# Feed-forward part of a decoder layer: up and down projection in one block, glu split into own buffers, last k steps by row tile

## What is computed

```python
def conv_glu_ffn(xn, w_up, conv_w, conv_b, w_down):
    h = causal_dwconv(xn @ w_up, conv_w) + conv_b      # 3 taps
    gate, val = jnp.split(h, 2, axis=-1)
    return (jax.nn.silu(gate) * val) @ w_down
...
        x = h + conv_glu_ffn(rms_norm(h, norm2_w[l]), ...)
    return rms_norm(x, final_norm_w)
```

## Time and profile before

| | us |
|---|---|
| median of 3 runs | 1781.9 |
| lowest, highest | 1780.5, 1782.3 |
| profiled execution: span | 1780.5 |
| profiled execution: its time, the lowest of the three | 1780.5 |
| TensorE busy in the span | 1693.2 (95%) |
| VectorE, ScalarE, GpSimd busy | 687.8, 494.3, 514.9 |

### The profile page before, as it was taken

How to read it: one execution, slowest core, us unless ns; L and a number is a source line. 1 busy time by engine, 2 the same in 40 slices (tenths; PEclk the granted TensorE clock), 3 DMA queues, 4 the chain that set the end, 5 groups by cost and what they waited for, 6 DMA issues and landing times. The chain is left out here.

```text
span 1780.5 us, 21145 instructions
## 1 busy us (share of the span) xinstructions
PE 1693.2 (95%) x8339; PEld 1408.3 (79%) x8339; DVE 687.8 (39%) x938; ACT 494.3 (28%) x617; POOL 514.9 (29%) x316
## 2 busy tenths in 40 slices
PE   6999999999999999996999789999999999799996
PEld 4788888887888888885788668888888888688885
DVE  4223223354454544642642313332222222345445
ACT  4322221222222343332221222222222222223223
POOL 4235231312213123212142322222222221344444
PEclk9999999999999999998899889999999999899998
DMA  4232422121121324432760111111111110311113
GB/s 156 60 95 71 136 82 58 40 56 53 48 67 44 91 79 112 132 117 102 253 235 34 62 48 47 47 47 47 48 54 51 47 47 24 130 50 50 47 47 124
DMA packets 173546, 139.64 MB, mean 78 GB/s; under 512 B 20420, under 2 KB 153004, under 8 KB 173484
## 3 DMA queue, kind: packets, MB, share of 16 engines
q1 hardware_dynamic: 173264, 138.67, 25.2%
q10 hardware_dynamic: 220, 0.09, 0.0%
HBM read 106.39 MB, written 32.34 MB: 78 GB/s over the span
## 5 line engine op out<-in xcount | busy, mean ns | idle before, releaser
L409 PE MATMUL acc<-xh,w_high 128*128 128x512 f32 x1504 | 486.3, 404 | 7.9 <-PEq L1376 7.9
L409 PE MATMUL acc<-xl,w_high 128*128 128x512 f32 x1504 | 468.8, 392 | 0.0
L409 PE MATMUL acc<-xh,w_low 128*128 128x512 f32 x1504 | 467.2, 391 | 0.0
L409 PEld LDWEIGHTS acc<-xl,w_high 128*128 128x128 f32 x1504 | 284.2, 189 | 61.1
L409 PEld LDWEIGHTS acc<-xh,w_low 128*128 128x128 f32 x1504 | 283.7, 189 | 61.4
L409 PEld LDWEIGHTS acc<-xh,w_high 128*128 128x128 f32 x1504 | 272.9, 190 | 64.1 <-issue 15.8
L1730 DVE SCALAR_TENSOR_TENSOR u_conv<-acc,prm,u_conv 128x1023 f32<-128x1023 f32 x88 | 112.8, 1282 | 341.1 <-ACT u_conv L1693 334.8
L779 POOL TENSOR_TENSOR w_low<-w_raw,w_high 128x1024 fp32r<-128x1024 f32 x49 | 117.0, 2388 | 376.5 <-ACT w_high L853 376.5
L1717 POOL TENSOR_TENSOR w_low<-w_raw,w_high 128x1024 fp32r<-128x1024 f32 x42 | 101.0, 2404 | 363.3 <-ACT w_high L1675 363.3
L1869 DVE TENSOR_TENSOR w_low<-w_raw,w_high 128x512 fp32r<-128x512 f32 x42 | 104.9, 2497 | 129.3 <-ACT w_high L1833 129.3
L1854 POOL TENSOR_TENSOR xl<-glu,xh 128x1024 fp32r<-128x1024 f32 x44 | 105.2, 2393 | 156.8 <-ACT xh L1830 131.6
(11 more groups left out here) (288 smaller groups left out, 2182.4 us busy)
## 6 DMA issues: line engine op xcount, KB each, us to landing
w_raw<-in_w_in_dram SPq DMA_DIRECT2D x51, 512.0 KB, 4.5
w_raw<-in_w_up_dram SPq DMA_DIRECT2D x44, 512.0 KB, 3.8
w_raw<-in_w_down_dram SPq DMA_DIRECT2D x44, 256.0 KB, 2.6
conv_d<-so SPq DMA_DIRECT2D x16, 512.0 KB, 3.0
gate_d<-qk SPq DMA_DIRECT2D x16, 512.0 KB, 3.1
g_gates<-gate_d SPq DMA_DIRECT2D x8, 1024.0 KB, 5.6
qk<-in_x_dram SPq DMA_DIRECT2D x8, 512.0 KB, 8.3
ckqk<-conv_d SPq DMA_DIRECT2D x8, 512.0 KB, 5.1
```

The lines of the kernel that those rows point to most:

```text
L409: mm = nc.tensor.matmul(out[:, lo:hi], w, xx[:, lo:hi], start=first and j == 0, stop=last and j == 2)
```

## The change

The functions `ffn`, `ffn_up`, `ffn_down` and `down_slots` become one `ffn` with one block.

- The order in which the operands of the down steps are prepared is a list `prep` of 44 (half, kk); `pos` gives a step's number in it, counted from 1: half 0's steps are 1 to 22, half 1's steps 0 to 13 are 23 to 36, and then steps 14 to 17 alternate with 18 to 21.
- `gh` and `gl` get buffers of their own (two slots each); the tail's (half 1, steps 18 to 21) lie in `xh`. The weights have four slots of a quarter of the ring each; the tail's lie in consumed tiles of `glu`. The rows of h lie in the memory of `xl`.
- ScalarE makes `gh` of steps 0 and 1 ahead of its last turn of up, and their weights' high parts inside it. VectorE makes their low parts between the two tap groups of the last turn.
- TensorE does steps 0 and 1 first on the row tiles whose banks are free (4 to 7, then 0 and 1), then on 2 and 3, and raises `s_k` for step 0 only then. Steps 18 to 21 of half 1 are done row tile by row tile, 12 matmuls each.
- The weights' split stands ahead of the glu split of the same number in ScalarE's queue; before, it stood behind. VectorE makes the low parts up to number `pos[(1, 2)]` = 25 ahead of half 0's additions.
- The squares of half 0's 512 columns go in ScalarE's queue at steps 2 to 9 of half 1, the product of these columns with the norm weight in GpSimd's at steps 6 to 13. At the end the square and VectorE's scaling are of 512 columns; ScalarE scales the other 512. Each row tile is stored in two halves.
- All loops over down steps are written out on all five engines.

```diff
+    prep = [(0, kk) for kk in range(FT)] + [(1, kk) for kk in range(BODY - GROUP)]
+    for pair in zip(lead, tail):
+        prep += pair
+    pos = count(prep)
...
+        gh2 = sb(ctx, "f_gh", [P, 2, S], F32R)
+        gl2 = sb(ctx, "f_gl", [P, 2, S], F32R)
...
+        def wait_used(eng, n):
+            if n == FT - 1:
+                eng.wait_ge(s_bank, NT)
+            else:
+                eng.wait_ge(s_k, n + 1 if n < FT else n)
...
             def _(sp):
...
+                for p in range(1, len(prep) + 1):
+                    load(p)
+                    if 5 <= p < 5 + NT:
+                        st = p - 5
+                        if st == 0:
+                            sp.wait_ge(s_acc, 2 * FT)
+                        sp.dma_start(h[st], h_d[...]).then_inc(s_h, 16)
...
+                for st in range(NT):
+                    sp.wait_ge(s_y2, st + 1)
+                    sp.dma_start(rows[:, 1, :], h[st][:, 1, :]).then_inc(s_out, 16)
+                    sp.wait_ge(s_y, st + 1)
+                    sp.dma_start(rows[:, 0, :], h[st][:, 0, :]).then_inc(s_out, 16)
...
             def _(act):
...
+                def glu_high(p):
+                    half, kk = prep[p - 1]
+                    n = half * FT + kk
+                    if half == 0:
+                        act.wait_ge(s_glu, kk + 1)
+                    if (half, kk) not in tail and n >= 2:
+                        wait_used(act, n - 2)
...
+                    nc.scalar.activation(gh(half, kk), glu[:, kk, :], ACT.Copy).then_inc(s_gh, 1)
...
+                glu_high(1)
+                glu_high(2)
                 turn(FT - 1, last=True)
+                for p in range(3, len(prep) + 1):
+                    down_high(p)
+                    glu_high(p)
+                    if prep[p - 1][0] == 1 and 2 <= prep[p - 1][1] < 2 + NT:
+                        square(0, prep[p - 1][1] - 2)
+                for st in range(NT + 1):
+                    if st < NT:
+                        square(1, st)
+                    if st:
+                        scale_first(st - 1)
...
             def _(pool):
...
+                for p in range(1, len(prep) + 1):
+                    pool.wait_ge(s_gh, p)
+                    nc.gpsimd.tensor_tensor(gl(half, kk), glu[:, kk, :], gh(half, kk).bitcast(F32),
+                                            ALU.subtract).then_inc(s_gl, 1)
+                    if half == 1 and 6 <= kk < 6 + NT:
...
+                        nc.gpsimd.tensor_tensor(h[st][:, 0, :], h[st][:, 0, :], fw[:, 0, :], ALU.mult).then_inc(s_first, 1)
...
             def _(dve):
...
+                taps(FT - 1, 0)
+                down_low(1)
+                down_low(2)
+                taps(FT - 1, 1)
+                gated(FT - 1)
+                early = pos[(1, 2)]
+                for p in range(3, early + 1):
+                    down_low(p)
+                dve.wait_ge(s_h, 16 * NT)
+                for st in range(NT):
+                    add(0, st)
+                for p in range(early + 1, len(prep) + 1):
+                    down_low(p)
...
+                for st in range(NT + 2):
+                    if st < NT:
+                        add(1, st)
+                    if 1 <= st <= NT:
+                        mean_square(st - 1)
+                    if st >= 2:
+                        scale_second(st - 2)
...
             def _(pe):
...
+                free = [st for st in range(NT) if st not in (2, 3)]
+                for kk in range(2):
+                    ready(0, kk)
+                    for st in sorted(free, key=lambda st: (st < 4, st)):
+                        if kk == 0 and st == 0:
+                            pe.wait_ge(s_taken, 2 * FT - 1)
+                        down(0, kk, st)
+                pe.wait_ge(s_taken, 2 * FT)
+                for kk in range(2):
+                    for st in (2, 3):
+                        mm = down(0, kk, st)
+                    mm.then_inc(s_k, 1)
...
+                            if half and kk == 0:
+                                pe.wait_ge(s_sum, st + 1)
+                            mm = down(half, kk, st)
...
+                for st in range(NT):
+                    for _, kk in tail:
+                        mm = down(1, kk, st)
+                    mm.then_inc(s_bank, 1)
```

More of the change, by code:

```diff
@@ L1624, in _ @@
                 transposes(NT - 1)
[L1627 to L1637, removed]
@@ L1649, in ffn_up @@
     with ExitStack() as ctx:
+        glu_at = nc.sbuf_base
+        glu = sb(ctx, "glu", [P, FT, S])
         cv = sb(ctx, "u_conv", [P, 2, S])
         sg = sb(ctx, "u_silu", [P, S])
+        gh2 = sb(ctx, "f_gh", [P, 2, S], F32R)
+        gl2 = sb(ctx, "f_gl", [P, 2, S], F32R)
+        ss0 = sb(ctx, "f_ss0", [P, 8])
+        FW_TILE, W_TILE = 2, 4
+        rows_of_h = nc.alloc_sbuf_tensor_at("f_h", [P, NT, NHALF, HALF], F32, offset=xl_at)
+        h = [rows_of_h[:, st] for st in range(NT)]
+        last_w = nc.alloc_sbuf_tensor_at("f_last_w", [P, GROUP, 2, HALF], F32R, offset=glu_at + W_TILE * S * 4)
@@ L1695, in turn @@
                         if j == 0:
-                            if not last:
+                            if last:
+                                down_high(1)
+                                down_high(2)
+                            else:
                                 split(i + 1, 0)
@@ L1741, in turn, with down_low @@
                                             ALU.mult).then_inc(s_glu, 1)
[L1743 to L1748, removed]
+                def down_low(p):
+                    half, kk = prep[p - 1]
+                    dve.wait_ge(s_dhi, p)
+                    nc.vector.tensor_tensor(dlo(half, kk), draw(p), dhi(half, kk).bitcast(F32),
+                                            ALU.subtract).then_inc(s_dlo, 1)
@@ L1761, in turn, with down, ready @@
                         mm.then_inc(s_acc, 1)
+                def down(half, kk, st):
+                    rows = slice(st * P, (st + 1) * P)
+                    a, b = gh(half, kk), gl(half, kk)
+                    for n, (x, w) in enumerate(((a, dhi(half, kk)), (a, dlo(half, kk)), (b, dhi(half, kk)))):
+                        mm = nc.tensor.matmul(every[st], x[:, rows], w, start=kk == 0 and n == 0,
+                                              stop=kk == FT - 1 and n == 2)
+                    return mm
+                def ready(half, kk):
+                    pe.wait_ge(s_gl, pos[(half, kk)])
+                    pe.wait_ge(s_dlo, pos[(half, kk)])
                 turn(0, True)
@@ new lines, in _ @@
+                for half in range(NHALF):
+                    for kk in range(0 if half else 2, BODY if half else FT):
+                        ready(half, kk)
+                        for st in range(NT):
+                            if half and kk == 0:
+                                pe.wait_ge(s_sum, st + 1)
+                            mm = down(half, kk, st)
+                            if not half and kk == FT - 1:
+                                mm.then_inc(s_bank, 1)
+                        if half or kk < FT - 1:
+                            mm.then_inc(s_k, 1)
```

289 lines of the change are left out of this document (122 added, 167 removed).

## The result

The changed kernel takes 1772.7 us (median of 4 runs, 1768.8 to 1773.2) against 1781.6 (median of 4 runs of the kernel before); the ratio is 0.9947, with a 95% interval of 0.9935 to 0.9958. That is faster by 0.5%, and 8.9 us against the 9.8 that the sum gave.

The account below looks back on a forecast made before the run. TensorE never rests inside the down projection, so only the joints can move: -10.4 + 1.7 + 5.1 + 1.9 - 8.1 = -9.8, from 1781.9 to 1772.1 us; own range 1769 to 1775, 8-in-10 range 1765 to 1777.

Parts of the forecast that it names:

- The turn: From up to down projection: no wait there, a new gap of 2.56 us before step 2; 10.4 us less.
- The clock in this gap: Slow TensorE clock from the new gap before step 2: 1.7 us more, bounds 0 and 3.4.
- The half change: From half 0 to half 1: TensorE waits behind ScalarE's weight split, VectorE's low part and first addition; 5.1 us more.
- The clock behind it: Half clock after the wait between half 0 and half 1: 1.9 us lost, bounds 0 and 3.4.
- The rival without this wait: Half 0 to half 1: no stall, as number 25's weights are split earlier; 1765.1 us, chance 0.07.
- Half 1: Norm work added to ScalarE and GpSimd during half 1 costs TensorE nothing: 0 us.
- The worst case for GpSimd and VectorE in the last pairs: Last prepared pairs: VectorE held through two GpSimd instructions, a low part late; 3 us kept as bound, 0 taken.
- The end: After the last matmul: 7.4 us to the end of the span instead of 15.5; 8.1 us less.
- The rival on the slower side: Down's written-out matmul stream: instructions come too slowly, pitch 0.24 us adds 14.0 us; 1786.1 us, chance 0.03.

Follow-up runs that it names:

- The two cuts: Changed kernel with VectorE's additions put before low part 25, 1763.7 us; or with ScalarE splitting weights 25 ahead of glu split 24, 1764.0 us.
- step 0 whole: Changed kernel, but TensorE does step 0 on all eight row tiles before step 1; 1768.5 us.
- tail by step: Changed kernel, but the last four k steps of half 1 go step by step over all row tiles; 1776.3 us.
- norm whole at the end: Changed kernel, but squares, scaling and store of all 1024 columns at the end, no norm work in half 1; 1773.4 us.
- late glu split: Changed kernel, but the glu splits of steps 0 and 1 stand behind ScalarE's last turn of up; 1775.3 us.

## Why the prediction was right

- **The turn.** Right. Step 2 starts 13.1 us behind up's last evacuation; the prediction had 1526.05 - 1512.82 = 13.2. The wait before it was 2.28 as recorded and 1526.14 - 1523.70 = 2.44 by slots, for 2.56 worked out from slots. One reading was off: 1536.48 is a time of the chain, whose pieces follow each other without the overlap of the matmuls. In the timeline the third step of the kernel before starts at 1536.32 (row below), so the forecast for the turn was worth 10.3 and not 10.4. The experiment with step 0 done whole shows that the late step counter is the cause of the wait.
- **The clock in this gap.** The term of 1.7 was 1.6 in the profiled run, but as a sure loss it was wrong, and that it came out is in part luck: the same wait was followed by half clock in four profiled runs and by full clock in two. The Trainium skill, page "TensorE: Matmul & The Clock Gate", section "What's actually happening", has the gate go by recent activity on a free-running beat; the six runs agree with that in so far as the same wait had either outcome, 14 or 21 matmuls behind it. The changed kernel's lowest run (1768.8, granted clock 0.982, the others 0.980) may have been spared too, but it has no trace, and it lies 4 us under the others, more than this one stretch can give.
- **The half change.** Right in mechanism and size: a wait of 4.96 by slots for 5.1, with each row of the chain in the forecast order. The two cuts show it. The clock behind it cost 2.5, not 1.9: the half clock lasted until 1646.9, 5.2 us behind the restart, where the row that the term came from had 3.7. This term is the largest miss of the sum. The rival without this wait, which had 0.07, is out.
- **Half 1.** Nothing was forecast and nothing was lost; the windows with and without the moved norm work are alike (115.1 us busy of 115.1, x509 both times). The worst case for GpSimd and VectorE in the last pairs (3 us) did not occur.
- **The end.** 7.3 us behind the last matmul for 7.4 forecast, so 8.2 less instead of 8.1. The chain was right to 0.3 us (the last store is issued at 4.1, not 4.4, since an issue took 0.33 to 0.52 and not 0.61). What the prediction did not say, and the experiments show, is which part pays: the spacing of the tiles.
- **The straight code.** The rival on the slower side is out. TensorE is busy for 105.6 us of 105.6 in half 0, and the matmuls did not come more slowly: from the third step on, the kernel before needs 1764.58 - 1536.32 = 228.26 us for 1007 starts, 0.2267 each, and the changed kernel starts its 48 matmuls of steps 0 and 1 in 1523.70 - 1512.82 = 10.88, also 0.2267 each.

The row that replaces 1536.48 (timeline, before):

```profile
1536.32 0.39 PE L1920 MATMUL acc<-w_high,xh 128*128 128x512 f32 x1
```

The sum with measured sizes: step 2 at 1526.14 - 1513.02 = 13.12 against 1536.32 - 1512.82 = 23.50 is -10.38. From there to the last matmul of half 0 the changed kernel needs 1636.47 - 1526.14 = 110.33 us for 479 starts, where 0.2267 each gives 108.59, so the clock in the gap is 1.74: the 1.6 and a second matmul that starts 0.34 us behind the first instead of 0.23. Then -10.38 + 1.74 + 4.96 + 2.54 - 8.20 = -9.34, and the distances give -9.3. The forecast of -9.8 was near because each of its terms was near. Its largest miss, 0.6 too little for the clock at the half change, was in part made good by 0.1 at the wait there and 0.1 at the end.

## What to carry to other kernels

When a prepared item is put early in a queue, follow it back to the engine that feeds it: VectorE's additions stood behind a low part that stood behind a copy that waited for the very half whose end the additions were to follow, and one index (25 for 24) cost 7.5 us in the profiled runs. A counter that frees a buffer should rise with the work that read it, not with the last piece of a reordered pair of steps. At the end of a kernel, space the last results so that the slowest consumer keeps up; after that, halving the consumer's work is worth little.

## What the runs showed of the hardware

- An idle of TensorE of 2.28 us in a dense stream was followed by half clock in four of six profiled runs (1.6 us lost each time, 14 matmuls in 4.8 us instead of 21) and by full clock in the other two. In the changed kernel the clock was still full for 1.4 us after the restart and fell then.
- A wait of 4.8 us in a dense stream was followed by half clock in all five profiled runs that have it (changed kernel, step 0 whole, tail by step, norm whole at the end, late glu split). By the time from the restart to the last matmul it cost 2.0 to 2.9 us.
- A VectorE subtraction of 512 columns took 0.68 us with GpSimd idle (1518.04) and 2.42 us with a GpSimd subtraction running beside it (1638.50).
- Profiled runs of kernels with the same code up to there reach up's last evacuation between 1511.2 and 1513.9 us, so a comparison of spans alone carries up to 2.7 us that the change has no part in.
- Half of a store's columns did not halve its time to the end: from the last issue to the end of the span it was 1771.4 - 1768.2 = 3.2 us for 256 KB in the changed kernel and 1780.5 - 1777.0 = 3.5 for 512 KB in the kernel before.
